# Down projections of ten segments by seven half-size products for eight, with the tokens stationary

## The reference

```python
def conv_ffn(h, up, conv_w, conv_b, down):          # D_FF = 5632
    hid = causal_dwconv(h @ up, conv_w, conv_b)     # up: 2048 x 11264
    gate, val = jnp.split(hid, 2, axis=-1)
    return (jax.nn.gelu(gate) * val) @ down         # down: 5632 x 2048
...
    y = conv_ffn(h, ffn_up, ffn_conv_w, ffn_conv_b, ffn_down)
    x = x + rms_norm(y, post_ffn_norm)
```

## Time and profile before

| | |
|---|---|
| median of three runs | 2678.56 us |
| profiled execution | 2675.24 us, span 2673.4 us |
| granted TensorE clock, mean | 0.999 |
| busy: TensorE | 2659.4 us (99%) |
| busy: VectorE | 1718.8 us (64%) |
| busy: ScalarE | 1042.9 us (39%) |
| busy: GpSimd | 256.0 us (10%) |
| quads of the up projections | about 1365 to 2175 us |
| down projections of ten segments | 2175 to 2611 us |
| last segment and closing norm | 2611 to 2673 us |

### The profile page before, as it was taken

How to read it: one execution, slowest core, us unless ns; L and a number is a source line. 1 busy time by engine, 2 the same in 40 slices (tenths; PEclk the granted TensorE clock), 3 DMA queues, 4 the chain that set the end, 5 groups by cost and what they waited for, 6 DMA issues and landing times. The chain is left out here.

```text
span 2673.4 us, 39595 instructions
## 1 busy us (share of the span) xinstructions
PE 2659.4 (99%) x17248; PEld 2322.1 (87%) x17248; DVE 1718.8 (64%) x1853; ACT 1042.9 (39%) x1094; POOL 256.0 (10%) x275
## 2 busy tenths in 40 slices
PE   9999999999999999999999999999999999999999
PEld 8778877877888888788889999999999988888888
DVE  6557467773554665623988778777777775545455
ACT  5335255632422333422654444444444432222215
POOL 1003100350000000011010000000000000000034
PEclk9999999999999999999999999999999999999999
DMA  6225311452232211233377777777777653333342
GB/s 232 87 87 197 126 64 66 155 183 91 85 110 87 98 68 66 94 128 110 142 198 188 192 205 192 194 203 189 198 205 186 185 173 120 117 126 111 126 159 94
DMA packets 95594, 376.85 MB, mean 141 GB/s; under 512 B 7216, under 2 KB 52400, under 8 KB 58048
## 3 DMA queue, kind: packets, MB, share of 16 engines
q1 hardware_dynamic: 77776, 271.76, 28.7%
q0 software_dynamic: 17360, 102.31, 16.6%
q10 hardware_dynamic: 288, 0.27, 0.0%
HBM read 342.86 MB, written 28.31 MB: 139 GB/s over the span
## 5 line engine op out<-in xcount | busy, mean ns | idle before, releaser
L1717 ACT ACTIVATE w_hi<-raw 128x2048 fp32r<-128x2048 f32 x145 | 277.3, 1912 | 695.3 <-PE ps L1618 331.5
L2411 DVE TENSOR_TENSOR w_lo<-raw,w_hi 128x2048 fp32r<-128x2048 f32 x145 | 339.8, 2343 | 249.8 <-ACT w_hi L1717 249.7
L876 PE MATMUL ps<-h_hi,w_hi 128*128 128x512 f32 x1200 | 481.5, 401 | 0.0
L878 PE MATMUL ps<-h_hi,w_lo 128*128 128x512 f32 x1200 | 468.1, 390 | 0.0
L877 PE MATMUL ps<-h_lo,w_hi 128*128 128x512 f32 x1200 | 467.7, 390 | 0.0
L1600 PE MATMUL ps<-h_hi,w_hi 128*128 128x256 f32 x1280 | 362.4, 283 | 0.9 <-DVE w_lo L3305 0.9
L1601 PE MATMUL ps<-h_lo,w_hi 128*128 128x256 f32 x1280 | 362.2, 283 | 0.0
L1602 PE MATMUL ps<-h_hi,w_lo 128*128 128x256 f32 x1280 | 362.2, 283 | 0.0
L876 PEld LDWEIGHTS ps<-h_hi,w_hi 128*128 128x128 f32 x1200 | 225.3, 188 | 57.4 <-issue 11.1
L878 PEld LDWEIGHTS ps<-h_hi,w_lo 128*128 128x128 f32 x1200 | 225.2, 188 | 48.2
L877 PEld LDWEIGHTS ps<-h_lo,w_hi 128*128 128x128 f32 x1200 | 225.6, 188 | 45.2 <-issue 1.9
(11 more groups left out here) (511 smaller groups left out, 5013.7 us busy)
## 6 DMA issues: line engine op xcount, KB each, us to landing
raw<-weights SPq DMA_DIRECT2D x172, 1024.0 KB, 4.8
raw<-weights POOLq DMA_DIRECT2D x40, 1024.0 KB, 8.3
X<-weights SPq DMA_DIRECT2D x39, 1024.0 KB, 6.4
q_raw<-weights SPq DMA_DIRECT2D x20, 1024.0 KB, 5.2
q_raw<-weights POOLq DMA_DIRECT2D x20, 1024.0 KB, 8.0
f_spill<-f_val POOLq DMA_DIRECT2D x22, 512.0 KB, 5.1
f_raw<-f_spill SPq DMA_DIRECT2D x10, 1024.0 KB, 6.9
x_spill<-X POOLq DMA_DIRECT2D x8, 1024.0 KB, 8.9
```

The costliest lines, as they stand in the source:

```text
L876: pe.matmul(o, w_hi[:, s % 2, w], h_hi[:, t, :], start=(t == 0), stop=False)
L878: mm = pe.matmul(o, w_lo[:, s % 2, w], h_hi[:, t, :], start=False, stop=(t == 15))
L1717: A(w_hi[:, slot, :], raw[:, slot, :], ACT.Copy).then_inc(w_hi_ready, 1)
L2411: V.tensor_tensor(w_lo[:, slot, :], raw[:, slot, :], w_hi[:, slot, :].bitcast(F32), ALU.subtract).then_inc(w_ready, 1)
```

## The change

The ten segments ahead of the last are taken in five pairs (`CHUNKS`). A pair's down projection is a product of f (512 tokens x 1024) by weights (1024 x 2048). It is done in two quads (numbers 20 to 29 follow the 20 of the up projections), each of seven products where eight were. Here the tokens stand still, in blocks of 128, and 512 columns of weights move, so that a product has 2 x 4 x 3 = 24 matmuls of 512 columns, and the result has tokens on partitions.

- The weight sums are made as in the up quads. The four sums of f (`form_1` to `form_4`) are made by GpSimd for each pair, split by ScalarE (`form_hi_made`, `form_hi_block`) and VectorE (`form_lo_made`, `form_lo_block`).
- Each of the seven products has its own running sum for even and odd quads (`acc`). ScalarE copies the first pair's products there, VectorE adds the others (`take`). After the last pair VectorE combines the seven (`mix`).
- The combined results are transposed on TensorE in eight groups of eight (`turn_out`) between tiles of the last segment. ScalarE copies half of them, VectorE adds the other half.
- The last segment is cut 256 and 256. ScalarE copies its first half from PSUM (`keep`) where VectorE added.
- x is no longer scaled where it is read back at the end. In quads 21 to 28 GpSimd loads two tiles of it a quad into one buffer, `x_tile`, scales each and stores it again; four plain transfers (`x_again`) bring it back beside the last segment.
- The last group of hidden channels' gate is multiplied by GpSimd in quad 20 (`gate_last`) where VectorE did it.

```diff
...
+        CHUNKS = (SEGS - 1) // 2
+        ALL_QUADS = QUADS + 2 * CHUNKS
+        U_LAST = U_UPS + PRODUCTS * ALL_QUADS
...
+        F_FORMS = ((t1_hi[:, 0:4, :], t1_hi[:, 4:8, :]), (h_hi[:, 0:4, N1], h_hi[:, 4:8, N1]), (h_hi[:, 0:4, N2], h_hi[:, 4:8, N2]),
+                   (h_hi[:, 8:12, N1], h_hi[:, 12:16, N1]), (t3_hi[:, 0:4, :], t3_hi[:, 4:8, :]),
+                   (X_r[:, 0:4, N1], X_r[:, 8:12, N1]), (h_hi[:, 8:12, N2], h_hi[:, 12:16, N2]))
...
+        Z_PLACE = ((J_A12, J_S4), (J_A22, J_S1))
+
+        TURNS = ((0, 0), (0, 1), (1, 0), (1, 1), (0, 2), (0, 3), (1, 2), (1, 3))
...
+        E1, E2 = N1, N2
+        E_LEN, E_BLOCK = (S // 2, S // 2), (128, 128)
...
+                if q >= QUADS and q % 2 == 0:
+                    c = (q - QUADS) // 2 + 1
+                    sp.wait_ge(*form_ready.at(4 + 7 * c))
+                    load_f(f_even[:, :, :], 2 * c)
+                    if c < CHUNKS:
+                        load_f(f_odd[:, :, :], 2 * c + 1)
...
+            def form_1(c):
+                pool.wait_ge(w_used, at(QUADS + 2 * c - 1, J_S1) + 2)
+                pool.wait_ge(f_landed[0], F_LANDED + 16 * (c + 1))
+                nc.gpsimd.tensor_tensor(F_RAW[J_S1], f_block(c, 0, 0), f_block(c, 0, 1),
+                                        ALU.subtract).then_inc(form_made.sem, 1)
...
+            def load_x(t):
+                pool.wait_ge(f_stored, X_STORED + 16 * t)
+                pool.dma_start(x_tile[:, :], x_spill2[:, t, :]).then_inc(sem("x_back"), 16)
+
+            def scale_x(t):
+                pool.wait_ge(*x_factor.at(2))
+                pool.wait_ge(sem("x_back"), X_BACK + 16 * (t + 1))
+                nc.gpsimd.tensor_tensor(x_tile[:, :], x_tile[:, :], rstd_k[:, :], ALU.mult).then_inc(sem("x_scaled"), 1)
+                pool.wait_ge(sem("x_scaled"), t + 1)
+                pool.dma_start(x_spill2[:, t, :], x_tile[:, :]).then_inc(f_stored, 16)
+
+            for q in range(QUADS, ALL_QUADS):
+                t = 2 * (q - QUADS - 1)
+                sum_q(q)
+                if 0 <= t < KT:
+                    load_x(t)
+                sum_r2(q)
+                if 0 <= t < KT:
+                    scale_x(t)
+                if 0 <= t < KT:
+                    load_x(t + 1)
+                if q % 2 and q < ALL_QUADS - 1:
+                    form_1((q - QUADS + 1) // 2)
+                    form_2((q - QUADS + 1) // 2)
+                if q == QUADS:
+                    gate_last()
+                    store_f(QUADS + 1)
+                    pool.wait_ge(f_stored, X_STORED)
+                if 0 <= t < KT:
+                    scale_x(t + 1)
+                if q % 2 and q < ALL_QUADS - 1:
+                    form_3((q - QUADS + 1) // 2)
+                    form_4((q - QUADS + 1) // 2)
...
+            def x_again(k):
                 pool.dma_start(x_back[:, 4 * k:4 * k + 4, :], x_spill2[:, 4 * k:4 * k + 4, :]).then_inc(sem("x_back"), 16)
-            pool.wait_ge(*x_factor.at(1))
-            pool.wait_ge(sem("x_back"), 128)
-            for t in range(16):
-                nc.gpsimd.tensor_tensor(x_back[:, t, :], x_back[:, t, :], rstd_k[:, :], ALU.mult).then_inc(sem("x_scaled"), 1)
+
+            pool.wait_ge(f_stored, X_STORED + 16 * KT)
+            pool.wait_ge(*mixed.at(7))
+            x_again(1)
+            pool.wait_ge(*turned_out.at(4))
+            x_again(2)
+            x_again(3)
+            pool.wait_ge(*mixed.at(14))
+            x_again(0)
...
+            def down_quad(q):
+
+                c = (q - QUADS) // 2
+                for j in range(PRODUCTS):
+                    n = at(q, j)
+                    pe.wait_ge(w_ready, n + 3)
+                    if q % 2 == 0:
+                        pe.wait_ge(*form_ready.at(4 + 7 * c + FORM_READY[j]))
+                    bank_taken(*divmod(PRODUCTS * q + j - 4, PRODUCTS))
+                    hi, lo = F_FORMS[j]
+                    o = pair(q, j)
+                    for a in range(2):
+                        tokens = slice(128 * a, 128 * a + 128)
+                        for k in range(4):
+                            w = slice(512 * k, 512 * k + 512)
+                            pe.matmul(o[:, a, :], hi[:, k, tokens], w_hi[:, n % 2, w], start=(k == 0), stop=False)
+                            pe.matmul(o[:, a, :], lo[:, k, tokens], w_hi[:, n % 2, w], start=False, stop=False)
+                            mm = pe.matmul(o[:, a, :], hi[:, k, tokens], w_lo[:, n % 2, w], start=False, stop=(k == 3))
+                    mm.then_inc(w_used, 1)
...
+            def turn_out(k):
+
+                n, g = TURNS[k]
+                if k < 2:
+                    bank_taken(ALL_QUADS - 1, J_S4 if k == 0 else J_S3)
+                else:
+                    before, g2 = TURNS[k - 2]
+                    pe.wait_ge(*(turn_copied if before else turn_added).at(g2 + 1))
+                pe.wait_ge(*mixed.at(7 * (g // 2) + 7))
+                src = acc(g // 2, Z_PLACE[g % 2][n])
+                o = turn_bank(k)
+                for t in range(4):
+                    for a in range(2):
+                        mm = turn(o[:, t, 128 * a:128 * a + 128], src[:, a, 128 * t:128 * t + 128])
+                mm.then_inc(turned_out.sem, 1)
...
+                            for k in {(0, 1, 3): (0, 1), (0, 2, 3): (2, 3), (0, 3, 3): (4, 5), (1, 0, 1): (6, 7)}.get((half, q, j), ()):
+                                turn_out(k)
...
+            def form_hi_made(c, j, n):
+                act.wait_ge(*form_made.at(4 + 4 * c + n))
+                A(F_FORMS[j][0], F_RAW[j], ACT.Copy).then_inc(form_hi.sem, 1)
+
+            def form_hi_block(c, j, k, n):
+                act.wait_ge(w_used, at(QUADS + 2 * c - 1, j) + 2)
+                act.wait_ge(f_landed[k], F_LANDED + 16 * (c + 1))
+                A(F_FORMS[j][0], f_block(c, k, n), ACT.Copy).then_inc(form_hi.sem, 1)
+
+            def take(q, j):
+                if q < QUADS + 2:
+                    act.wait_ge(w_used, at(q, j) + 2)
+                    if (q, j) == (QUADS + 1, J_S1):
+                        act.wait_ge(f_stored, X_STORED)
+                    A(acc(q % 2, j), product(q, j), ACT.Copy).then_inc(taken_act.sem, 1)
+
+            def down_quad(q):
+                c, p = divmod(q - QUADS, 2)
+                act.wait_ge(*r_summed[q % 2].at(16 * (q // 2 + 1)))
+                hi(at(q, J_S1), raw[:, q % 2, :])
+                if p == 0:
+                    form_hi_made(c, J_S3, 3)
+                if q > QUADS:
+                    take(q - 1, J_A22)
+                act.wait_ge(*q_landed.at(16 * (q + 1)))
+                hi(at(q, J_A11), q_raw[:, :])
+                if p == 0:
+                    form_hi_made(c, J_A22, 4)
+                    form_hi_block(c, J_S4, 1, 1)
+                if q == QUADS:
+                    val_tap0(q - 1)
+                else:
+                    take(q - 1, J_S4)
+                act.wait_ge(*summed.at(q + 1))
+                hi(at(q, J_S2), raw[:, q % 2, :])
+                if q == QUADS:
+                    gate_tap0(q - 1)
+                if p == 1 and c + 1 < CHUNKS:
+                    form_hi_made(c + 1, J_S1, 1)
+                take(q, J_S1)
+                act.wait_ge(*a12_landed.at(16 * (q + 1)))
+                hi(at(q, J_A12), a12_at(q))
+                take(q, J_A11)
+                if p == 1 and c + 1 < CHUNKS:
+                    form_hi_block(c + 1, J_A11, 0, 0)
...
+            def take(q, j):
+                if q >= QUADS + 2:
+                    dve.wait_ge(w_used, at(q, j) + 2)
+                    V.tensor_tensor(acc(q % 2, j), acc(q % 2, j), product(q, j), ALU.add).then_inc(taken.sem, 1)
...
+                lo(at(q, J_S1), raw[:, q % 2, :])
+                if q == QUADS:
+                    finish_val(q - 1)
+                else:
+                    take(q - 1, J_A22)
+                if p == 0:
+                    form_lo_made(c, J_S2, 3)
+                dve.wait_ge(*q_landed.at(16 * (q + 1)))
+                V.tensor_tensor(raw[:, q % 2, :], raw[:, q % 2, :], q_raw[:, :], ALU.add).then_inc(summed.sem, 1)
+                lo(at(q, J_A11), q_raw[:, :])
...
+            for t in range(12):
+                keep(t)
+                if t in (1, 5):
+                    step_hi_end(N_POS - 2 + t // 4)
+                if t == 9:
+                    for n in range(4):
+                        end_square(0, n)
+            turn_in(2)
+            turn_in(3)
...
```

More of the change, by code:

```diff
@@ L615, in _, with load_f @@
             load_a22(0)
-            for q in range(QUADS):
+            def load_f(dst, seg):
+                sp.wait_ge(f_stored, F_STORED + 32 * (seg + 1))
+                sp.dma_start(dst, f_spill[:, 4 * seg:4 * seg + 4, :]).then_inc(f_landed[seg % 2], 16)
+            for q in range(ALL_QUADS):
+                if q == QUADS - 1:
+                    sp.wait_ge(w_used, at(q, J_S1) + 2)
+                    load_f(f_even[:, :, :], 0)
                 sp.wait_ge(w_ready, at(q, J_A12) + 3)
```

(51 more changed lines are left out.)

433 lines of the change are left out of this document (263 added, 170 removed).

## The result

| | median, us | runs | span of the profiled execution | granted clock |
|---|---|---|---|---|
| before | 2677.93 | 4 (2675.35 to 2678.57) | 2673.4 | 0.999 |
| after | 2716.17 | 4 (2715.71 to 2717.20) | 2713.9 | 0.985 |

The ratio is 1.0147 (95% interval 1.0132 to 1.0162): 38 us slower. I had forecast 2698 (2666 to 2714): the side was right, the size too small by 18 us, and the time lies 2 us outside the range.

A forecast was written before the change was run, and what follows sets the result against it. TensorE was taken to set the end until the tail, unless another engine is late. Terms: 2675.24 - 54.4 + 53.6 + 1.0 + 6.8 + 3 + 1 + 12 = 2698.2 us, slower; range 2666 to 2714.

The forecast's parts named there:

- Products: Down projections of the ten segments: 1680 matmuls instead of 1920, 5.44 us a product, 54.4 us saved.
- Four waits: Quads 21, 23, 25, 27: TensorE waits 13.4 us each for A12's weights, behind ScalarE's copy of GpSimd's late difference; +53.6.
- The 1.0 of quad 21: Quad 21: ScalarE also copies a product there, adding 1.0 us to the wait.
- Clock: After each of the four waits: TensorE's clock at half for some 3 us, 1.7 lost each; +6.8 (0 to 10).
- Even quads: VectorE between the differences for S1 and A11: 0.3 beyond slack plus GpSimd beside it, 0.8 four times; +3 (0 to 8).
- Handover: Quad 19, forms of f copied and low parts written ahead of S4's weights: 2 us of wait for 0.9; +1 (0 to 3).
- End: Last segment to the end: 64 transposes on TensorE +8.6, waits and late squares +3.4; together +12.
- the tile's transfers pass the accumulations: Rival, GpSimd's DMA queue: waits of 7.2 us, four times 28.8; 2665, or 2673 with all terms; chance 0.17.
- the waits don't show: Rival, the odd quads' waits: none visible, the change gives what the count says, 2637; chance 0.08.
- VectorE and GpSimd on top: Rival, pairs of quads: DMA engines or differences excluding each other cost 2 to 5 more a pair, 2706 to 2720; chance 0.15.
- The DMA engines: Same rival's other half: some 69 of 76 us busy in two quads, late loads adding 2 to 5 a pair; chance 0.15.

The follow-up runs named there:

- the first run: Changed kernel with GpSimd forming S1's difference before the first tile load and S2's before the second: 2660.6 us, ratio to before 0.9944.
- the last one on the copies: Changed kernel with ScalarE's copy of S1's form behind A22's weights, the copies for S2 and A12 behind S4's: 2681.2 us.
- the combined run: Changed kernel with differences ahead of tiles, handover reordered with GpSimd held back, last gelu behind A22's weights, second-half squares beside gains: 2649.3 us, ratio to before 0.9906.
- that run: Changed kernel with ScalarE squaring the second half's tiles beside the first half's gains, instead of all sixteen gains first: 2710.4 us.

## Why the prediction was right and where it was wrong

- **Products, -54.4.** Right: 5.44 us each, all 1680 counted.
- **Four waits, +53.6 and +1.0.** Right in place and cause: from product to product, 12.15 + 12.19 + 14.08 + 15.35 = 53.8. That the sum fits within 1 us is luck. I had four equal waits; the first two are shorter, since raw's accumulation landed at +7.5 instead of +8.8 and the difference took 2.35 instead of 2.9. The later ones are longer because the accumulation for the quad after next is issued late and stands in the queue too (in quad 27, 3.6 us ahead of q_raw's), which I hadn't counted. The 1.0 of quad 21 is there: ScalarE begins A12's copy 1.86 us after t_hi's, in quad 23 0.97. It doesn't show in the wait, because quad 23's w_lo takes 2.98 for 2.29, beside GpSimd. The order alone is shown to be the cause by the first run, and ScalarE's queue as its carrier by the last one on the copies.
- **Clock, +6.8.** Undersized: the products behind the waits took 7.27, 8.23, 7.48 and 8.01 for 5.44, so 9.2 in four. In 2252 to 2256 us the clock is 0.50 and in 2256 to 2259 it is 0.90; in quad 23 it is still 0.54 in 2346 to 2349.
- **Even quads, +3.** Right in size, 0.8 in quads 24, 26 and 28, 2.35 in sum; quad 22 has none. Quad 20's 2.4 I had missed: there the last gelu, which waits for VectorE's taps, stands ahead of the copy of A22's weights. It is the same form as the forecast wait, in the one place where I hadn't looked. In the combined run, where it stands behind, that wait is gone.
- **Handover, +1. This step failed.** The down quads begin 8.7 later. Of that 0.75 is already there ahead of the handover (w_lo at 2159.44, before at 2158.69); the rest is a wait of 6.2 for 0.9, and 2.7 of low clock up to 2181.8. I had counted VectorE's instructions at their durations alone, while three of GpSimd's four forms lie beside them (2161.90 to 2172.09). The Trainium skill (SBUF — State Buffer, "Who interferes with whom") has a VectorE instruction with two inputs in SBUF contend with a GpSimd instruction that reads it. By that rule the trace agrees: 1.21 apart, 3.4 beside. In the forecast I weighed the rule against one row, 0.9 more for a w_lo, took the row's size, and used it for the even quads only. In that row GpSimd has short instructions (1.54) one after another and VectorE a single one, which waits out one turn at most. Where both engines have one instruction after another they alternate, and each instruction takes nearly the sum of both, 3.4 where 1.21 and 2.35 make 3.56.
- **End, +12. This step failed too.** It took 18.3 more. The transposes cost 7.0 (four groups of 1.75), not 8.6. The waits are 0.9 + 1.7 + 4.8 = 7.4, where I had 3.4, and the stretch from the last sum to the end is 18.2 where it was 13.9 (2659.51 to 2673.4). In the combined run it is 15.4 (2631.01 to 2646.4) with the clock at 1.00 in its first five microseconds. By this comparison some 2.8 of the 4.3 are low clock behind the last wait, which I hadn't counted; it is an estimate, as the order of the gains differs too, and no run shows what the other 1.5 are. I had put the end of the squares about 2 us behind the last tile. Sixteen gains stand ahead of them (2674.71 to 2681.2), so that the first begins at 2681.11, 4.6 us after its tile was added (2676.51; not 7 us late, as the expectation of that run has it), and GpSimd, at 1.0 each beside VectorE where the earlier trace rows has 0.69, never caught up.
- **The rivals.** That the tile's transfers pass the accumulations is refuted by the landing times (7.9 us for a quarter of a MB, 0.7 behind the accumulation issued ahead of it). That the waits don't show, too. "VectorE and GpSimd on top" was the right addition, but not in the pairs of quads, where the long waits gave room: it sat at the handover. It takes its place in the quads as soon as the waits are gone. The DMA engines weren't the bound: in the down quads of the changed kernel no copy of weights on ScalarE waits for a transfer.

By the sum: 2698.2 + 7.7 (start of the down quads) + 6.3 (end) + 3.6 (the ten quads took 448.9 where the terms make 445.3: more for the clock and quad 20, a little less for the waits and the even quads) = 2715.8; the profiled execution took 2715.7.

Open: why one wait of 2.3 us without the tiles left the clock whole, while two others lowered it; and which part of the 11.6 us left in the combined run a better placing could still take. Neither was tried.
